# A hybrid decoder layer on eight cores: more DMA semaphores, constants first, plain products for q and k in the first supertile, the next norm applied beside the down projection

## What is computed

```python
h  = rmsnorm(x, norm_mix_gain)
q_a, k_a, v_a, q_r, k_r, v_r, g_r, z_a, z_r = split(h @ w_in)
A  = sliding_window_attention(q_a, k_a, v_a)          # window 128, q/k norm, sinks
R  = silu(g_r) * rms_group_norm(retention(q_r, k_r, v_r))  # chunks of 128, decaying state
m  = sigmoid(z_a) * (A @ w_branch_attn) + sigmoid(z_r) * (R @ w_branch_ret)
x  = x + m @ w_out
h  = rmsnorm(x, norm_ffn_gain)
x  = x + (silu(h @ w_gate) * (h @ w_up)) @ w_down
```

## Time and profile before

| | us |
|---|---|
| median of 3 runs | 5470.93 (5458.59 to 5474.81) |
| the profiled execution's own time | 5455.77 |
| span of its slowest core (core 2) | 5453.9 |
| other cores of that execution | 5407.0 to 5445.5 |
| TensorE busy in the span | 5073.1 (93%) |
| VectorE, ScalarE, GpSimd busy | 3130.1, 2704.9, 1639.0 |

### The profile page before, as it was taken

One profiled execution on the slowest core, in us unless ns is written; L12 is line 12 of the kernel. 1 busy time (PEld: TensorE's weight loads), 2 busy tenths in 40 slices (PEclk: granted clock), 3 DMA queues, 4 the chain that ended last, 5 costly groups with the idle time before them and its releaser, 6 DMA issues.

```text
span 5453.9 us, 65097 instructions; the slowest of 8 cores (5407.0 to 5453.9 us)
## 1 busy us (share of the span) xinstructions
PE 5073.1 (93%) x24179; PEld 2226.1 (41%) x24666; DVE 3130.1 (57%) x4971; ACT 2704.9 (50%) x5026; POOL 1639.0 (30%) x1709
## 2 busy tenths in 40 slices
PE   6788889989999999999999999999999999999979
PEld 2333333434344443444334443444434443444434
DVE  5864788336863368633785348743587335853352
ACT  4482646335573365733656346653456435573231
POOL 2513353023620235202442035311262112620131
PEclk9999999999999999999999999999999999999989
DMA  8678679886669566675576754775647646557445
GB/s 199 190 204 171 199 206 242 224 183 218 195 204 247 156 214 215 203 213 181 173 244 206 198 185 157 255 226 172 222 157 228 216 135 207 182 178 219 138 167 158
DMA packets 433869, 1075.24 MB, mean 197 GB/s; under 512 B 164240, under 2 KB 225680, under 8 KB 421264
## 3 DMA queue, kind: packets, MB, share of 16 engines
q1 hardware_dynamic: 418144, 1013.90, 59.5%
q0 software_dynamic: 15408, 57.15, 6.7%
HBM read 847.84 MB, written 246.68 MB: 201 GB/s over the span
## 4 chain that ended last, share of the span: by engine, by line
PE 71%; DMA 14%; DVE 8%; ACT 4%; issue 2%; POOL 1%; SPq 0%; DVEq 0%; ACTq 0%; POOLq 0%
PE bk L420 70%; DVE sb L479 4%; ACT sb L456 4%; DMA sb<-wk 3%; DMA sb<-w 2%; DVE sb L488 2%; DMA sb<-x2s 2%; DMA sb<-rts 2%; DVE bk L479 1%; DMA sb<-x 1%; DMA ats<-sb 1%; DMA h1s<-sb 1%; DMA vs<-sb 1%; POOL sb L479 0%; DMA sb<-cf 0%
## 5 line engine op out<-in xcount | busy, mean ns | idle before, releaser
L420 PE MATMUL bk<-sb 128*128 128x512 bf16 (+1 forms) x23675 | 5052.5, 376 | 376.5 <-DVE sb L479 131.6
L420 PEld LDWEIGHTS bk<-sb 128*128 128x128 bf16 (+2 forms) x24162 | 2195.8, 99 | 3210.3 <-issue 359.5
L456 ACT ACTIVATE sb<-bk 128x512 f32<-128x512 f32 (+1 forms) x2828 | 1590.8, 597 | 1751.1 <-PE bk L420 1390.2
L479 POOL TENSOR_TENSOR sb<-sb 128x512 bf16<-128x512 f32 (+3 forms) x1090 | 1252.4, 1157 | 2814.9 <-DVE sb L488 1479.5
L479 DVE TENSOR_TENSOR sb<-bk,sb 128x512 f32<-128x512 f32 (+1 forms) x1360 | 894.4, 684 | 581.8 <-PE bk L420 418.3
L456 ACT ACTIVATE sb<-sb 128x512 f32<-128x512 f32 (+2 forms) x1364 | 823.2, 625 | 599.3 <-DMA sb<-x 193.1
L479 DVE TENSOR_TENSOR bk<-bk,sb 128x512 f32<-128x512 f32 x864 | 599.7, 696 | 593.8 <-PE bk L420 433.2
L488 DVE SCALAR_TENSOR_TENSOR sb<-sb,bk 128x512 f32<-128x512 f32 x752 | 499.8, 684 | 504.3 <-PE bk L420 503.7
L479 DVE TENSOR_TENSOR sb<-sb 128x512 bf16<-128x512 bf16 (+3 forms) x765 | 533.0, 724 | 200.0 <-DMA sb<-rts 81.1
L456 ACT ACTIVATE sb<-bk,sb 128x512 bf16<-128x512 f32 (+1 forms) x560 | 380.8, 688 | 322.1 <-POOL sb L479 142.7
L488 DVE SCALAR_TENSOR_TENSOR sb<-sb 128x1 f32<-128x1 f32 (+2 forms) x544 | 309.1, 590 | 295.7 <-ACT sb L456 218.4
(11 more groups left out here) (6 smaller groups left out, 23.7 us busy)
## 6 DMA issues: line engine op xcount, KB each, us to landing
sb<-wk SPq DMA_DIRECT2D x378, 896.0 KB, 5.8
sb<-x SPq DMA_DIRECT2D x128, 512.0 KB, 8.3
sb<-h1s SPq DMA_DIRECT2D x112, 512.0 KB, 9.6
sb<-x2s SPq DMA_DIRECT2D x224, 256.0 KB, 8.1
wk<-sb SPq DMA_DIRECT2D x54, 896.0 KB, 8.0
sb<-w POOLq DMA_DIRECT2D x71, 512.0 KB, 8.6
sb<-wk SPq DMA_DIRECT2D x48, 704.0 KB, 6.3
vs<-sb SPq DMA_DIRECT2D x256, 128.0 KB, 5.4
```

What stands on the lines that cost most here:

```text
L420: fns.append(lambda e, out=out, l=l, r=r, start=start, kw=kw: e.matmul(out.get(), l.get(), r.get(), start=start, stop=True, skip_group_che ...
L456: return e.activation(out.get(), in_.get(), func, scale=scale.get() if isinstance(scale, V) else scale, **kw)
L479: return self.op(eng, [lambda e: e.tensor_tensor(out.get(), a.get(), b.get(), op)], d, [a, b], [out], lock=lock, key=key)
```

## The change

It has ten parts. (1) 100 DMA semaphores on SP and 24 on POOL. (2) The constants are loaded before x; the first kv weights wait for two x tiles, not four. (3) The first supertile follows `ORDER`; its qa, k and q units use 8 plain products with the raw weights, and their weight sums and stored copies are made after the products. (4) Its token sums are made later; norm1 of supertile 1 and the loads of the rotation tables wait for the first qa unit. (5) `keep_at` spreads the storing of copies: kv and v in supertile 1, z in 1 or 2, the retention branch in 2. (6) `norm1_apply` of s+1 uses the q/k area Q and is due 180 us (virtual) behind the start of F(s-1). (7) The retention is spread over 165 us (virtual), not 190. (8) In the last supertile x2 stays in SBUF. (9) Its norm2 runs in the order in which two interleaved gu units (`group2`) need the blocks. (10) In supertile 0 some PSUM copies go to ACT in place of DVE.

```diff
-    def __init__(self, nsp=24, npq=12, nact=0):
+    def __init__(self, nsp=100, npq=24, nact=0):
...
+ORDER0 = ORDER
+PLAIN0 = "kq"
...
-        B.cur.vt = -1e6
+        B.cur.vt = -3e6
         B.dma("sp", cst.get(), cf_d, NCONST * 512, [], [cst])
...
         def keep_at(name):
-            return min(1 if name[0] in "bd" else 0, ns - 1)
+            if name[0] == "z":
+                w = 1 + int(name[1:]) % 2
+            elif name[:2] == "br":
+                w = 2
+            else:
+                w = 1 if name[0] in "bdv" or name == "kv" else 0
+            return min(w, ns - 1)
...
+            if kind == "s" and s == 0 and name[0] in PLAIN0:
+                w, keep = wget(name, s, 0, True)
+                for fi, t in ((0, 0), (1, 0), (1, 1), (0, 1)):
+                    b = bank()
+                    mmgroup(b, w[RAW[2 * fi]] + w[RAW[2 * fi + 1]], hb[NB[2 * t]] + hb[NB[2 * t + 1]], True)
+                    cons(fi, t, b)
+                keep()
+                return
...
+        def group2(names, s, hb, conss):
+
+            a = []
+            for nm, cons in zip(names, conss):
+                w = wget(nm, s)
+                b1 = bank()
+                mmgroup(b1, w["A11"], hb["B11"], True)
...
+                mmgroup(b3, w["A12"], hb["B21"], True)
...
+                mmgroup(b4, w["S4"], hb["B22"], True)
...
+            for (w, b1, s3, cons) in a:
+                b2 = bank()
+                mmgroup(b2, w["S3"], hb["T3"], True)
...
+        def norm2_last(s):
+            hb = hblocks(YR(s + 1))
+            for (t, i) in ((0, 0), (0, 1), (1, 1), (1, 0)):
+                for q in range(4):
+                    B.stt("dve", hb[NB[2 * t + i]][q], f32(x2home(q, t) + 2 * KB * i), small("g2", q + 4 * i), nacc2[t],
+                          ALU.mult, ALU.mult)
+            for (o_, a, b) in (("T3", "B22", "B12"), ("T1", "B12", "B11"), ("T2", "B22", "T1"), ("T4", "T2", "B21")):
+                for q in range(4):
+                    B.tt("dve", hb[o_][q], hb[a][q], hb[b][q], ALU.subtract)
...
+                if s == ns - 1:
+                    x = f32(x2home(q, t) + 2 * KB * (m >= 4))
+                else:
+                    x = t32()
+                    B.dma("sp", x.get, x2_d[s, q, :, j, :], 256 * KB, [x2k[s, q, t]], [x], key=B.cur.vt - 6000)
...
+            if s == 0 and ns > 1:
+                on(Stream(B, va, 1.0, "s"))
+                st = norm1_squares(1, T + 12 * KB, 20000.0, (p0,))
...
+                norm1_apply(1, (YR(0) + 24 * KB,), None, ve - va - 30000.0, (p0,))
...
-            if 0 < s < ns - 1:
-                B.tag = f"n{s + 1}"
-                on(Stream(B, dense.vt + 20000.0, 1.0, "s"))
-                norm1_apply(s + 1, (XR(s) + 24 * KB, T), (XR(s) + 20 * KB, T + 8 * KB), 60000.0)
-                on(dense)
             if s > 0:
-                phase_ret(s, 190000.0)
+                phase_ret(s, 165000.0)
+                if s < ns - 1:
+                    B.tag = f"n{s + 1}"
+                    on(Stream(B, dense.vt + 180000.0, 1.0, "s"))
+                    norm1_apply(s + 1, (Q, Q + 8 * KB), (Q + 16 * KB, Q + 24 * KB), 50000.0)
+                    on(dense)
                 phase_F(s - 1)
...
-        norm2(ns - 1, 10000.0)
+        norm2_last(ns - 1)
```

More of the change, by code:

```diff
@@ L771, in wget, with keep @@
                     B.ts("dve", bl[3], bl[3], -1.0, ALU.mult, key=k2)
[L772 to L775, removed]
+                if raw_ and not plain:
+                    sums(vt - 8000)
+                res = {nm: [b16(a + 256 * (n * i + k), 128) for k in range(n)] for i, nm in enumerate(RAW if plain else FIN)}
+            def keep():
+                if s == last and s < ns - 1 and not again:
+                    if plain:
+                        sums(B.cur.vt)
+                    kept[name] = V(None, (B.newcell(),), 0, True, False)
+                    B.dma("sp", kd, full.get(), 256 * nk, [full], [kept[name]], key=B.cur.vt + 8000)
+            if plain:
+                return res, keep
+            keep()
             return res
@@ L933, in norm1_first, with norm1_squares @@
                         B.stt("dve", hb[NB[j]][q], xt(q, j), small("g1", q + 4 * (j & 1)), nacc1[t], ALU.mult, ALU.mult)
[L934 to L941, removed]
+        def norm1_squares(s, base, span, after=()):
             v0 = B.cur.vt
@@ L950, in norm1_squares, with norm1_apply @@
             return st
-        def norm1_apply(s, qa, oa, span):
+        def norm1_apply(s, qa, oa, span, after=()):
             v0 = B.cur.vt
@@ L1288, in mblocks, with x2home @@
             return hb
+        def x2home(q, t):
+            n = 2 * q + t
+            return (A["W"] + 4 * KB * n) if n < 4 else (A["Db"] + 4 * KB * (n - 4)) if n < 6 else (Q + 4 * KB * (n - 5))
         def stage_o(s, st, q, hb):
@@ L1338, in cons, with stage_gu @@
                     B.tt("dve" if b.ps else "pool", acttile(s, f, t), a, b, ALU.mult)
-            group(f"gu{f}", s, hb, cons)
+            return cons
+        def stage_gu(s, hb, f):
+            group(f"gu{f}", s, hb, gucons(s, f))
         def stage_d(s, m):
@@ L1387, in phase_W @@
+            for st in (st2.get(s - 1), st1.get(s + 1)):
+                if st is not None:
                     st.finish(0)
                     st.finish(1)
[L1389 to L1422 removed]
@@ new lines, in phase_W @@
+            on(dense)
+            va = ve = p0 = None
+            for n, step in enumerate(ORDER0 if s == 0 else ORDER):
+                if n > 0 and late:
+                    store_x2(3)
+                if step == "kv":
+                    stage_kv(s, hb)
+                elif step[0] == "v":
+                    stage_v(s, hb, int(step[1]), int(step[2]) if len(step) > 2 else None)
+                elif step[:2] == "qa":
+                    stage_qa(s, hb, (int(step[2]),))
+                    p0 = p0 or lastpe()
+                    if step == "qa2":
+                        va = dense.vt
+                else:
+                    if step == "k0":
+                        load_cs(s, (p0,))
+                    stage_qk(s, hb, step[0], int(step[1]))
+                    if step == "q3":
+                        ve = dense.vt
@@ L1440, in phase_F @@
             hb = hblocks(YR(s + 1))
-            for f in range(22):
+            if s == ns - 1:
+                group2(["gu0", "gu1"], s, hb, [gucons(s, 0), gucons(s, 1)])
+            for f in range(2 if s == ns - 1 else 0, 22):
                 stage_gu(s, hb, f)
```

114 lines of the change are left out of this document (62 added, 52 removed).

## The result

The changed kernel takes 5501.57 us (median of 4 runs, 5487.86 to 5513.19), the kernel before 5469.91 (4 runs, 5458.59 to 5474.81): a ratio of 1.006, interval 1.0031 to 1.0089. It is slower by about 32 us, where 96 us less had been forecast. The profiled execution took 5505.56 us.

The account below looks back on a forecast made before the run. TensorE, at 93% of the span, was taken as the bound, with stretches where it idles or runs slowly. Terms summed to -96 us: from a median of 5471 to 5375 us, ratio 0.982, range 5325 to 5435.

Parts of the forecast that it names:

- The earlier retention issues nothing new: Retention in the F stages, spread over 165 us: costed at nothing, as the gate units hide it.
- F(0) and F(1) are full of transfers anyway: Next norm moved beside the down projection in F(0) and F(1): most cost only moves, -5 and -4 us.
- The slower one: Rival, chance 0.06: in F, x loads waiting for Q block SP's in-order queue; 24 us a supertile would give 5495 us.
- the third rival: Chance 0.10: raw weights on POOL's queue land late, none hidden, 31 + 45 us in place of 13; 5438 us.
- start: Kernel's beginning: constants ahead of x let the first half's norm follow its own four x tiles; -10 us.
- W(1): Supertile 1's projection stage: kv and v loaded raw through POOL, +5 us (0 to +12).
- W(0): First supertile's projection: later order, plain q and k; 197 us against 231.5, -34 us (-46 to -12).
- Z(1)+Z(2): Z stages of supertiles 1 and 2: raw z and branch loads, stores and sums, +8 us (0 to +20).
- Z(0): First supertile's Z stage: eight z copies fewer to store, 7.3 MB of 61.5 MB; -12 us (0 to -25).
- F(2)-F(5): Norm moved beside the down projection: each stage saves 10 us at its start, pays 4; -24 us (-40 to +10).
- the end: Between Z(7) and F(7): x2 kept in SBUF lets the first products start near 5208.2 us; -24 us (-28 to -16).
- semaphores: Closing waits at the kernel's end: 76 more at 0.05 us each, +4 us (0 to +4).

Follow-up runs that it names:

- E1: Changed kernel with the transposed loads of Z(1) to Z(7) held until the down projection ahead has ended; ratio to before 0.998, F(0) 312.2 us, F(1) 276.6.
- E3: Changed kernel with the retention spread over 190 us again; ratio to before 1.0005, F(0) 314.2 us, F(1) 273.1.
- E2: Changed kernel with the next norm back at the start of F in its old buffers, retention still 165 us; F(0) 312.0 us, F(1) 289.7, no ratio.
- E7: Changed kernel with retention over 190 us, old rule for storing copies, and transposed loads held until the down projection ended; ratio to before 0.9933.
- E4: Changed kernel with weight copies stored by the old rule (branch and down weights in supertile 1, others in 0); ratio to before 1.0022.
- E12: Changed kernel with retention 190 us, old copy rule, held transposed loads, 24 and 12 semaphores, norm at its old place; median 5420.6 us, ratio to before 0.9917.
- E10: Changed kernel with copies of the down weights stored in supertile 2; F(2) 293.5 us, F(1) 275.6, no ratio.
- E11: Changed kernel with retention over 190 us, old copy rule, held transposed loads, and 24 and 12 semaphores again; ratio to before 0.9945.
- E8: Changed kernel with copies of the down weights stored in supertile 0, not 1; cores 0 to 3: F(1) 257.6 us, F(0) 361.0, no ratio.

## Why the prediction was wrong

**The step that failed** is "The earlier retention issues nothing new, and I cost it at nothing: the gate units hide it, as they do now." From F(2) on the earlier retention does cost nothing by itself. But its end releases the transposed loads of Z(s+1): nothing new is issued, something is issued earlier, into the stretch of F(0) and F(1) that has raw down weights (in F(1) stores of their copies too) and now the norm. F(0) and F(1) came out at +35.3 and +23.4 us where -5 and -4 were forecast, 68 of the 137 us by which the sum was wrong. E1 and E3 each return 44 to 46 us of the two, but not in the same place. Split at the first gate product and the first down product ("down": up to Z's first product), on the mean core:

```
us                   before  after    E1     E3     E2
                                     hold  ret190  norm
F(0) wait for gates     5.9   12.4   11.0   11.9   13.3
F(0) gates            195.9  217.9  217.8  204.4  207.5
F(0) down              99.0  105.7   83.4   97.9   91.2
F(1) wait and gates   175.4  178.2  176.8  170.4  181.9
F(1) down              98.0  118.7   99.8  102.8  107.7
```

The shift of the retention alone takes 5 us from the down part and gives them to the gates (as in F(2) to F(5) below). E1 returns 22 and 19 us, in the down parts: that is the transposed loads' cost, and part of it was there before the change (E7). E3 returns 8 and 16 there. But most of F(0)'s +35 arises earlier, before any transposed load is issued: 6.5 in the wait, which E4 takes away, and 22 in the gates. There E3 returns 13.5 (5 of them the shift) and E2 10.4, and with both undone (E12, which has the old rule for copies too) it is 194.5: the faster retention costs time in F(0)'s gate part too, and so does the moved norm. The gate part repeats well, 217.9 us here and 217.0 in E10; the down part does not, 105.7 and 100.2. So a second step failed beside the first, "F(0) and F(1) are full of transfers anyway (0.95 and 0.81), so most of it only moves". The sign of being wrong that the prediction named, down projections of 98 us, did come in F(0) and F(1), but on the mean core it had stood there before (99.0 and 98.0).

**The rivals.** The slower one named the place, SP's queue standing still in F beside the down projection, and not the cause. The first x load of each F did wait for Q, and SP issued nothing for 5 to 8 us before it (cores 0 and 3), but in the gate part; beside the down projection it was 1.2 us at most. There a transfer held SP while it was being issued. E2 still loses in F(1) with none of the norm's x loads there. Nor is it the rule of the Trainium skill weighed in the third rival (DMA: Bandwidth & Descriptors, section SWDGE vs HWDGE vs iDMA), that VectorE, in one of its modes, locks GpSimd out: the late down weight was issued at 988.67 us, and VectorE is busy 2.36 and 0.00 us in the two stretches of 20 us in which 35 and 47 GB/s are moved. The prediction's 14.0 against 6.2 us is no sign for that rule either: the raw loads read float32, twice the bytes of the copies.

**Term by term**, on the mean core, forecast and measured:

```
start          -10    -9      W(1)        +5    +7      F(0), F(1)  -5, -4   +35, +23
W(0)           -34   -16      Z(1)+Z(2)   +8   +22      F(6)             0        +5
Z(0)           -12    -3      F(2)-F(5)  -24    -9      the end        -24       -29
semaphores      +4    +4      Z(3)-Z(6)    0   +10
```

*Start*: right. *W(0)*: right in kind, half the size. VectorE's share fell to 69% (146.64 of 211.80). But the 924 matmuls took 189.6 us, not 183, at a granted clock of 0.96, and 22 us of idle time remain instead of the 14 in my 197, most of it for ScalarE. Part (10) gave it copies, but that part was not tried alone, and before the change TensorE waited 15.1 us for ScalarE in W(0) already (waits by releaser, 24 to 236 us: total, count, longest):

```profile
PE bk L420 <- ACT sb L456: 16.9, 8, 5.6
```

*Z(0)*: transfer time saved there was not TensorE's; E4 puts the stores back at no cost to Z(0). *W(1), Z(1), Z(2)*: the sign was right; E4 shows 7 and 19 us, so two stages of raw z and branch weights cost more than twice my 8.

*F(2) to F(5)*: TensorE's wait at the start of F did go. Before the first gate product it waited 5.9, 6.0, 4.1 and 4.4 us on the mean core, afterwards 0.6 to 0.9. The 10 us taken were read on the slowest core, and the mean wait was 5.1. And the norm's cost is not where I looked: the down projection of F(2) to F(5) is 80.5 us instead of 85.6 and the gate part 175 instead of 169.5, which is the retention's shift alone (168 and 85.5 again in E3). It shows in Z(3) to Z(6), +10, of which E2 returns 7. The gate stages of these four took 193.5 us before, 199.7 in the changed kernel and 194.7 in E2; that the moved norm ends later and pushes work into them is likely, but was not shown. E11 against E12 says that in sum moving it saves nothing (it costs 10 us there; the two ratios overlap).

*The end*: right, also in its steps. VectorE's and TensorE's timeline between Z(7) and F(7), to be held against the earlier trace rows:

```profile
5278.48 1.14 ACT L456 ACTIVATE sb<-sb 128x512 f32<-128x512 f32 x2
5279.14 10.69 DVE L488 SCALAR_TENSOR_TENSOR sb<-sb 128x512 bf16<-128x512 f32 x16 [1.94 <-ACT sb L456]
5282.02 7.97 PE L420 MATMUL bk<-sb 128*128 128x512 bf16 x28 [4.16 <-DVE sb L488]
5289.75 5.45 DVE L479 TENSOR_TENSOR sb<-sb 128x512 bf16<-128x512 bf16 x16
5294.00 18.35 PE L420 MATMUL bk<-sb 128*128 128x512 bf16 x84 [1.74 <-DVE sb L479]
```

*Semaphores*: right, 100 closing waits take 5.4 us, 0.05 each as in the earlier trace rows (line, count, first and last start):

```profile
L1607 SPq EVENT_SEMAPHORE  x100: 17/17/17, 5497.9 to 5503.3; - x100
```

**Open.** What carries the loss of F(0)'s gate part, a transfer or an engine, was not told apart, only that the faster retention and the moved norm share it. Why raw loads and transposed loads are slow together was not found either, only that they are. Parts (2) to (4) and (8) to (10) were not tried alone.

## What to carry to other kernels

A stage that ends earlier releases everything that waits for it. Before costing an earlier end at nothing, list the transfers that it frees, see in the trace when they will go out and what is in flight there; a due time does not hold a transfer back, a dependence does. A stall seen on the slowest core should be averaged over the cores before it is multiplied by the number of stages.

## What the chip showed that was not expected

A transposed load held the issuing engine for 25 to 33 us (F(0), core 3; 16 to 29 on the mean core) when raw weights were being cast on their way in through POOL's queue, and 4 to 9 us beside plain copies (E8's F(1) and the changed kernel's F(2), 8.93 and 4.15 us there):

```profile
2405.20 8.93 SPq L514 DMA_TRANSPOSE sb<-rts  x1
...
2415.24 4.15 SPq L514 DMA_TRANSPOSE sb<-rts  x1
```

Meanwhile the transfer engines count as busy (share 1.28 to 1.33) and move 35 to 47 GB/s. The Trainium skill (Advanced Engine Details and Errata, section X-Bar Transpose (TRN2)) says that transposing transfers are as fast as regular ones. Over the whole execution the trace agrees: the median landing of the 64, of 512 KB each, is 6.0 us, where the 64 plain loads of that size shown here take 5.3. Beside raw loads it does not: there the two in F(0) took 27 and 62 us on core 3, and raw loads of 704 KB a median of 48.9 us (14.1 on E1's core 6, where no transposed load is beside them). Transfers of the changed kernel by kind (count, KB each, median us to landing), whole execution and then 960 to 1083 us:

```profile
sb<-vs SPq DMA_DIRECT2D x64, 512.0 KB, 5.3
...
sb<-rts SPq DMA_TRANSPOSE x64, 6.0
...
sb<-w POOLq DMA_DIRECT2D x4, 704.0 KB, 48.9
```
